# A transformer stack on one core: heads of the hybrid layers reordered, modulation pieces spread over later projections, first attention one step deeper

## The reference, cut to what matters

```python
for l, mixer in ((0, diff_attention), (1, neighbourhood_attention)):
    mod = silu(c) @ ada_w[l] + ada_b[l]          # six rows of 1024 channels, for x and for the context
    x += gate * mixer(rmsnorm(x) * (1 + scale) + shift)      # qkv, attention, wo
    x += gate * conv_ffn(rmsnorm(x) * (1 + scale) + shift)   # up, depthwise conv, silu gate, down

def _diff_attend(q, k, v, lam, subln, lam_init):  # 8 heads of two halves j
    s = jnp.einsum('bqhjd,bkhjd->bhjqk', q, k).astype(jnp.float32) * (HEAD_DIM ** -0.5)
    p = jax.nn.softmax(s, axis=-1)
    a = (p[:, :, 0] - lam * p[:, :, 1]).astype(v.dtype)
    o = jnp.einsum('bhqk,bkhe->bqhe', a, v)
    o = rmsnorm(o, subln) * (1.0 - lam_init)

for l in range(2):                                # hybrid layers
    h = rmsnorm(x, norm_g[l]); proj = h @ w_in[l]
    o = nsa_mixer, pool_mixer, conv_mixer, fox_mixer  of slices of proj
    acc = sum(sigmoid(merge[i]) * ((o[i] * silu(gates[i])) @ w_branch[i]) for i in range(4))
    x = x + acc @ w_out
```

## Time and profile before

| what | value |
|---|---|
| device time, median of 3 | 1682.14 us (1679.67 to 1682.47) |
| the profiled execution's own time | 1682.3 us |
| its span | 1680.5 us |
| mean granted clock of PE | 0.987 |
| busy PE, DVE, ACT, POOL | 1609.4, 893.8, 748.7, 539.6 us |

### The profile page before, as it was taken

One profiled execution on the slowest core, in us unless ns is written; L12 is line 12 of the kernel. 1 busy time (PEld: TensorE's weight loads), 2 busy tenths in 40 slices (PEclk: granted clock), 3 DMA queues, 4 the chain that ended last, 5 costly groups with the idle time before them and its releaser, 6 DMA issues.

```text
span 1680.5 us, 26674 instructions
## 1 busy us (share of the span) xinstructions
PE 1609.4 (96%) x10956; PEld 1404.1 (84%) x10956; DVE 893.8 (53%) x1405; ACT 748.7 (45%) x1359; POOL 539.6 (32%) x359
## 2 busy tenths in 40 slices
PE   6999988999999999999999999998999998999997
PEld 4769556778777888868968999997999998999997
DVE  3344485347523564333165788647575557568334
ACT  4323475345322343234276655445544444554443
POOL 1224144223211222220273111024424665523553
PEclk8999999999999999999999999999999999999999
DMA  9165510344255222366233454553534543533551
GB/s 395 54 228 182 204 64 1 141 147 156 68 203 201 100 77 69 121 213 230 81 76 133 151 190 160 173 177 120 196 125 155 176 168 119 201 126 131 181 191 51
DMA packets 52984, 249.39 MB, mean 148 GB/s; under 512 B 20608, under 2 KB 21760, under 8 KB 26368
## 3 DMA queue, kind: packets, MB, share of 16 engines
q1 hardware_dynamic: 44400, 244.42, 41.9%
q10 hardware_dynamic: 8464, 3.28, 0.8%
HBM read 246.63 MB, written 1.05 MB: 147 GB/s over the span
## 4 chain that ended last, share of the span: by engine, by line
PE 86%; DVE 7%; ACT 2%; DMA 2%; issue 2%; POOL 1%; SPq 0%; POOLq 0%; DVEq 0%; ACTq 0%
PE psq L529 18%; PE psq L531 17%; PE psq L530 17%; PE ps L529 6%; PE ps L531 6%; PE ps L530 6%; PE ps L542 2%; DMA RAW<-wstream 2%; PE psq L884 1%; PE psq L885 1%; PE psq L886 1%; DVE STAT L1154 1%; PE ps L1290 1%; ACT WH L501 1%; PE psq L2105 1%
## 5 line engine op out<-in xcount | busy, mean ns | idle before, releaser
L511 DVE TENSOR_TENSOR WL<-RAW,WH 128x1024 fp32r<-128x1024 f32 (+3 forms) x263 | 316.9, 1229 | 413.4 <-ACT WH L501 413.4
L529 PE MATMUL psq<-NH,WH 128*128 128x256 f32 (+1 forms) x1640 | 521.9, 318 | 13.3 <-DVE TMP L1727 10.9
L531 PE MATMUL psq<-NH,WL 128*128 128x256 f32 (+1 forms) x1640 | 515.5, 314 | 0.0
L530 PE MATMUL psq<-NL,WH 128*128 128x256 f32 (+1 forms) x1640 | 515.3, 314 | 0.0
L511 POOL TENSOR_TENSOR WL<-RAW,WH 128x1024 fp32r<-128x1024 f32 (+2 forms) x117 | 297.0, 2540 | 552.4 <-ACT WH L501 552.3
L501 ACT ACTIVATE WH<-RAW 128x1024 fp32r<-128x1024 f32 (+2 forms) x380 | 361.2, 1001 | 206.5 <-DMA RAW<-wstream 152.2
L529 PEld LDWEIGHTS psq<-NH,WH 128*128 128x128 f32 x1640 | 316.1, 193 | 42.8 <-DVE TMP L1727 11.2
L531 PEld LDWEIGHTS psq<-NH,WL 128*128 128x128 f32 x1640 | 315.7, 193 | 18.2
L530 PEld LDWEIGHTS psq<-NL,WH 128*128 128x128 f32 x1640 | 316.2, 193 | 17.3
L529 PE MATMUL ps<-NH,WH 128*128 128x256 f32 (+1 forms) x376 | 124.3, 331 | 0.0
L530 PE MATMUL ps<-NL,WH 128*128 128x256 f32 (+1 forms) x376 | 123.5, 328 | 0.0
(11 more groups left out here) (346 smaller groups left out, 2837.1 us busy)
## 6 DMA issues: line engine op xcount, KB each, us to landing
RAW<-wstream SPq DMA_DIRECT2D x196, 1024.0 KB, 4.9
RAW<-wstream SPq DMA_DIRECT2D x32, 704.0 KB, 4.1
K<-first SPq DMA_DIRECT2D x4, 1024.0 KB, 15.9
X<-xin SPq DMA_DIRECT2D x2, 1024.0 KB, 6.1
V<-first SPq DMA_DIRECT2D x2, 1024.0 KB, 19.7
Q<-first SPq DMA_DIRECT2D x2, 1024.0 KB, 25.2
BR<-rpb ACTq DMA_DIRECT2D x8, 256.0 KB, 9.0
BR<-rpb SPq DMA_DIRECT2D x8, 256.0 KB, 8.5
```

What stands on the lines that cost most here:

```text
L511: e.tensor_tensor(WL[:, u % 3, a:z], RAW[:, v % 3, a:z], WH[:, u % 3, a:z].bitcast(F32), ALU.subtract).then_inc(w_lo_p if pool else w_lo_v, 1)
L529: e.matmul(o, lh, rh, start=start, stop=False)
L530: e.matmul(o, lh, rl, start=False, stop=False)
L531: return e.matmul(o, ll, rh, start=False, stop=stop)
```

## The change

It touches orders and waits, and buffers in the first attention. (1) Start: the first row copy stands ahead of the split of unit 0, the second ahead of that of unit 1; the second part of the constants is loaded behind the fifth `first` unit. (2) First attention: jobs 0 to 3 compute scores among the last value tiles; every stage behind them has one age more (44 steps), with nine P tiles; five pieces of wo are used in its last steps. (3) Modulation units 4 to 7 of two groups stand between later projections, none in front of the first. (4) Heads of the hybrid layers: DVE copies kn right behind qn; the turns, the flats' split and the gain stand later. (5) POOL (and for two units DVE) make the last low weight parts behind low parts of activations; some wo units are split two ahead instead of three.

```diff
@@ -136,8 +136,8 @@
...
-UP_ADA = {("up", 0, 0): (0, 1, 2, 3, 4), ("up", 0, 1): (5,), ("up", 0, 2): (6,), ("up", 0, 3): (7,)}
-QKV_ADA = {("qkv", 1, 4): (0, 1, 2, 3, 4), ("qkv", 1, 5): (5,), ("qkv", 1, 6): (6,), ("qkv", 1, 7): (7,)}
+UP_ADA = {("up", 0, 0): (0, 1, 2, 3), ("up", 0, 2): (4,), ("up", 0, 3): (5,), ("up", 0, 4): (6,), ("up", 0, 5): (7,)}
+QKV_ADA = {("qkv", 1, 4): (0, 1, 2, 3), ("qkv", 1, 6): (4,), ("qkv", 1, 7): (5,), ("qkv", 1, 0): (6,), ("qkv", 1, 1): (7,)}
...
@@ -165,18 +165,18 @@
...
-    for i in range(3):
+    for i in range(2):
         add(("wo", 0, i), 1, run=False)
     for k in range(DT):
         add_ada(2, k)
         run_ada(2, k)
-    add(("wo", 0, 3), 1000, run=False)
+    for i in range(2, 4):
+        add(("wo", 0, i), 1000, run=False)
     runs += [("wo", 0, i) for i in range(4)]
     for j in range(HALF_FT):
         add(("up", 0, j), 2)
-        if j == 1:
-            for k in range(DT):
-                add_ada(3, k)
+        for k in {1: range(4), 2: (4,), 3: (5,), 4: (6,), 5: (7,)}.get(j, ()):
+            add_ada(3, k)
     for m in range(DT):
...
@@ -187,9 +187,8 @@
...
         add(("qkv", 1, i), 1000)
-        if i == 5:
-            for k in range(DT):
-                add_ada(5, k)
+        for k in {5: range(4), 6: (4,), 7: (5,), 0: (6,), 1: (7,)}.get(i, ()):
+            add_ada(5, k)
...
 
-            return SPLIT_AT[UNIT_OF[key]] + (3 if key[:2] in (("qkv", 0), ("wo", 0)) else 2)
...
                             pe_ada(e, 5, k)
-                    if u == 6:
+                    if u == 7:
...
                 for q in range(2):
-                    if l == 1 and i == 3:
-                        act_na_exp(e, q)
+                    if i == 3:
+                        (act_na_exp if l else act_diff_exp)(e, q)
                     e.wait_ge(gemm, product(key, q))
                     e.activation(V[l][:, 2 * q:2 * q + 2, 256 * i:256 * i + 256], pair(bank[b + q]),
                                  ACT.Copy).then_inc(v_sb, 1)
                 if l == 1 and i == 2:
                     e.activation(STAT[:, 11, 16:17], ONE, ACT.Exp)
-                if l == 0 or i < 3:
+                if i < 3:
                     split_hi(e, ahead(key))
...
-        DIFF_STEPS = 43
+        DIFF_STEPS = 44
...
+        def diff_p(j, i):
+
+            if i == 0:
+                return PP[:, j % 5, :]
+            return PP[:, 5 + j % 4, :] if j % 4 < 2 else TMP[:, j % 4, :]
+
+        def pe_diff_qk(e, j):
+            h, qt, k0, nk = diff_job(j)
+            if j < 2:
+                e.wait_ge(v_sb, 4 + 2 * j)
+            if j % 4 == 0:
+                e.wait_ge(qk_sb, 2 * (8 + h) + 2)
+                e.wait_ge(rot_v, 3 * (8 + h) + 3)
+            if j >= 2:
+                e.wait_ge(att_exp, 2 * (j - 1))
+            for i in range(2):
+                ps = slice(64 * i, 64 * i + 64)
+                e.matmul(bank[2 * (j % 2) + i][:, 0:nk], Q[0][ps, h, qt * P:qt * P + P], K[0][ps, h, k0:512],
+                         start=True, stop=True).then_inc(att_qk, 1)
...
             for n in range(DIFF_STEPS):
-                for age, j in each_step(n, 10, 32):
+                for age, j in each_step(n, 11, 32):
                     h, qt, k0, nk = diff_job(j)
-                    if age == 10 and qt == 3 and h < 7:
+                    if age == 11 and qt == 3 and h < 7:
                         pe_out_turn(e, h)
-                    if age == 5:
+                    if age == 6:
+                        if j == 0:
+                            e.wait_ge(v_sb, 8)
...
-                    if age == 4:
+                    if age == 5:
                         wait_mix(e, j)
+                        if j == 0:
+                            e.wait_ge(v_sb, 7)
                         if j >= 1:
...
+                    if age == 0 and j >= 4:
+                        pe_diff_qk(e, j)
...
-                if 33 <= n < 37:
+                if 33 <= n < 38:
...
+        def act_diff_exp(e, j):
+            h, qt, k0, nk = diff_job(j)
+            if j >= 4:
+                wait_mix(e, j - 4)
+            if j >= 5:
+                e.wait_ge(att_tr, j - 4)
+            e.wait_ge(att_max, j + 1)
+            for i in range(2):
+                e.activation(diff_p(j, i)[:, 0:nk], bank[2 * (j % 2) + i][:, 0:nk], ACT.Exp, bias=STAT[:, j % 8, i:i + 1],
+                             accum_out=STAT[:, j % 8, 2 + i:3 + i]).then_inc(att_exp, 1)
...
-                                         accum_out=STAT[:, j % 8, 2 + i:3 + i]).then_inc(att_exp, 1)
+                    if age == 1 and j >= 2:
+                        act_diff_exp(e, j)
...
+        def pe_last_values(e, l):
+
+            key = ("qkv", l, 11)
             v, wh, wl = weights(key)
             for q in range(4):
-                pe_na_qk(e, q)
+                (pe_na_qk if l else pe_diff_qk)(e, q)
                 if q == 0:
-                    e.wait_ge(v_sb, 10)
+                    e.wait_ge(v_sb, 8 * l + 2)
                 o = bank[4 + q // 2][:, 256 * (q % 2):256 * (q % 2) + 256]
...
                     if i == 3:
                         e.wait_ge(x_res, x_ready(1, 1))
                     if i == 0:
-                        pe_abreast(e, ("wo", l, i), [bank[b], bank[b + 1]], range(4, DT), wait_x)
+                        pe_abreast(e, ("wo", l, i), [bank[b], bank[b + 1]], range(5, DT), wait_x)
...
             n = 1 + 2 * l
             for i in range(4):
-                if l or i < 3:
-                    split_hi(e, ahead(("wo", l, i)))
+                split_hi(e, ahead(("wo", l, i)))
...
+                    last = (l, m) == (1, DT - 1)
                     for half in range(1 if l == 0 else 2):
                         key = ("down", l, c if l == 0 else half, m)
-                        split_lo(e, ahead(key), False)
+                        if not (last and half):
+                            split_lo(e, ahead(key), False)
...
                     dve_raw_lo(e, 0, DT - 1)
+                    split_lo(e, ahead(("down", 1, 1, DT - 1)), False)
...
                     for half in range(1 if l == 0 else 2):
+                        if (l, half, m) == (1, 1, DT - 1):
+                            e.wait_ge(raw_lo, 8)
                         split_lo(e, ahead(("down", l, c if l == 0 else half, m)), True)
...
             lo_prep(e, l, "qn", False)
             dve_raw_out(e, l, "qn")
+            lo_prep(e, l, "kn", False)
+            dve_raw_out(e, l, "kn")
...
         def act_head(e, l):
-            for kind in range(2):
-                if kind == 0:
-                    e.wait_ge(flat, 5 * l + 5)
-                f = FLT[:, kind, :].rearrange("p (k n) -> p k n", k=16)
-                e.activation(FHV[:, kind, :, 0, :], f, ACT.Copy).then_inc(flat_hi, 1)
             act_plain(e, l, "vn", VN[:, :, :])
...
             act_plain(e, l, "qf", QF[:, :, :], 0.125)
+            for kind in range(2):
+                if kind == 0:
+                    e.wait_ge(flat, 5 * l + 5)
+                f = FLT[:, kind, :].rearrange("p (k n) -> p k n", k=16)
+                e.activation(FHV[:, kind, :, 0, :], f, ACT.Copy).then_inc(flat_hi, 1)
             act_plain(e, l, "kf", KF[:, :, :])
...
             e.memset(FHL[:, 1024:1152].bitcast(U32), 0).then_inc(flat_lo, 1)
-            for kind in range(2):
-                f = FLT[:, kind, :].rearrange("p (k n) -> p k n", k=16)
-                e.wait_ge(flat_hi, 2 * l + kind + 1)
-                e.tensor_tensor(FHV[:, kind, :, 1, :], f, FHV[:, kind, :, 0, :].bitcast(F32),
-                                ALU.subtract).then_inc(flat_lo, 1)
-            e.memset(CM[:, 0:384].bitcast(U32), 0).then_inc(cm_zero, 1)
-            dve_turn(e, l, 0, QN[:, :, :])
-            lo_prep(e, l, "kn", False)
-            dve_raw_out(e, l, "kn")
-            dve_turn(e, l, 1, KN[:, :, :])
-            if l == 0:
-                dve_out_gain(e, 5, "nout")
             lo_prep(e, l, "vn", False)
...
             e.memset(LF[:, :, :].bitcast(U32), 0).then_inc(fx_v, 1)
+            dve_turn(e, l, 0, QN[:, :, :])
...
             e.tensor_scalar(GS, GS, 0.5, 0.5, ALU.mult, ALU.add).then_inc(gs_v, 1)
+            for kind in range(2):
+                f = FLT[:, kind, :].rearrange("p (k n) -> p k n", k=16)
+                e.wait_ge(flat_hi, 2 * l + kind + 1)
+                e.tensor_tensor(FHV[:, kind, :, 1, :], f, FHV[:, kind, :, 0, :].bitcast(F32),
+                                ALU.subtract).then_inc(flat_lo, 1)
+            e.memset(CM[:, 0:384].bitcast(U32), 0).then_inc(cm_zero, 1)
             lo_prep(e, l, "qf", False)
+            dve_turn(e, l, 1, KN[:, :, :])
             lo_prep(e, l, "kf", False)
+            if l == 0:
+                dve_out_gain(e, 5, "nout")
...
             if l == 0:
                 e.wait_ge(d_late, 16)
                 e.wait_ge(gemm, product(("down", 1, 1, 7)))
+            lo_prep(e, l, "kn", True)
             pool_turn(e, l, 0, QN[:, :, :])
```

(19 more changed lines are left out.)

68 lines of the change are left out of this document (21 added, 47 removed).

## The result

The changed kernel takes 1660.57 us (median of 4 runs, 1657.08 to 1661.6), the kernel before 1680.91 us (4 runs): the ratio is 0.9869, with a 95% interval from 0.985 to 0.9887, about 22 us less by the ratio. The profiled execution has a span of 1658.5 us, against 1680.5. That lies inside the stated range, and 12 us above the predicted 1649.

A forecast was written before the change was run, and what follows sets the result against it. PE's matmuls, busy 1609.4 of 1680.5 us, were taken to bound the kernel. Terms of -5.8, -12.3, -1.1, -8.0 and -5.5 summed to -32.7 us against 1682.3, giving 1649 us, with a range of 1638 to 1665.

The forecast's parts named there:

- the first rival: Whole kernel: attention stays at 11.05 us per head (+6.0), clock lost in the hybrid heads (+6.8); 1662 us, chance 0.20.
- The start: Row copies ahead of splits: waits -4.9, clock -3.3, new waits 2.4; sum -5.8, taken as -6 us.
- new wait for first pieces: At the start, PE arrives sooner and waits for the first units' weight pieces; put at 2.4 us.
- The first attention: Wait for first exponentials -3.3, half-clock stretch -3.0, head period 11.05 to 9.8 us for five heads -6.0; sum -12.3 us.
- I take no change there: End of the first attention: one more wo piece (k = 4) covers the last head's later chain; 0 us.
- My reason for the period: First attention: DVE's 9.93 us busy per head becomes longest, partly held by POOL, so a head takes 9.8 us.
- The norm passages: Modulation pieces no longer ahead of the projections: +0.8 after norm 1, -1.9 after norm 2; sum -1.1 us.
- The heads: Hybrid heads: kn wait of 5.51 us gone, new wait of about 4.4 at vf; -4.0 per layer, -8.0 us.
- 15, against 13.6: Hybrid heads, from vf to g1: the compress weights' split chain takes 15 us, before 13.6; g1 at 36.9.
- Before the out projection: POOL waits for the low sums, DVE's low splits shrink and all four PE waits go; -5.5 us.
- The rest at nothing: Later last splits of dve_ffn and dve_out, later wo splits, value loop with three splits: 0 us.
- The rival of the ring: Three weight buffers: modulation units between ten projections make PE wait for weights; above 1682, for example 1690 us, chance 0.02.

The follow-up runs named there:

- x7_start_old: Changed kernel with the old start: split of unit 0 ahead of the first row copy, tables' transfer behind the first weight unit; 1664.91 us, ratio to before 0.9895.
- x2_piece_back: Changed kernel with the fifth wo piece (k = 4) back behind the last step of the first attention; 1659.65 us, ratio to before 0.987.
- x1_turn_late: Changed kernel with PE turning a head's output at the end of the step in the first attention; 1660.27 us, ratio to before 0.9879.
- x8_ada_old: Changed kernel with modulation units 4 to 7 of both norm passages back in their old places; 1663.62 us, ratio to before 0.9884.
- x9_bias_sp: Changed kernel with four transfers of the second attention's bias block 1 issued by SP instead of ACT; 1657.56 us, ratio to before 0.9852.
- x5_heads_old: Changed kernel with the hybrid layers' heads in the old order on DVE, ACT and POOL; 1661.36 us, ratio to before 0.9868.
- x6_out_old: Changed kernel without POOL's wait for the low sums ahead of its weight split before the out projections; 1667.19 us, ratio to before 0.9904.
- x3_vf_early: Changed kernel with ACT's and DVE's splits of unit vf earlier in both hybrid heads; 1659.65 us, ratio to before 0.986.

## Why the prediction was right, and where its sizes were off

**The time.** The sum named 1649 and the time is 1660.57. That lies above what I called likeliest, 1641 to 1657, and nearest to the first rival's 1662; it is in the range because the range took in that rival. Of the rival's two causes one came, the clock lost in the heads, and the other did not: a head of the attention did not stay at 11.05 us. So the agreement with its number is partly luck.

**What bounds it.** Right: PE's work is unchanged, and the gain came out of waits, 19.2 of 22.0 us. The clock gave little as a whole, since the removed stretches were replaced by others: PE's busy time fell by 2.8 us, where the start and the attention alone were to give 6.3.

**The start.** Forecast -6, measured -5.6; x7_start_old confirms it at 5.7 by place. The new wait for first pieces was smaller than put (1.12 us, not 2.4), and the clock gave less back (0.84 over 14 to 35 us instead of 0.76, so 1.7 us and not 3.3).

**The first attention.** Forecast -12.3, measured -9.1 with the stretch ahead of it, 0.8 of which is the wait at 112. The wait of 3.32 us and the stretch at 0.50 are gone as forecast. The period was 10.06, where I said 9.8; that is 5.0 us for five heads instead of 6.0. The step that failed is "I take no change there": moving piece k = 4 into the last steps took a cover of 1.4 us from the last head's norm, so the wait grew from 1.07 to 2.45 us, and a stretch of 3.4 us at 0.51 came with it. x2_piece_back shows both. My reason for the period (DVE's 9.93 us of busy time) did not hold, although the number was near: that time fell to 8.51 with the change, and PE waits for POOL's norm, 1.20 us a head where it was 0.48, or in x1_turn_late for exponentials. DVE's instructions make up most of the chain there, so their order may be the limit; that is argued, not shown.

**The norm passages.** Forecast -1.1. The places of both traces say +1.1 at norm 1 (I took +0.8) and -0.9 at norm 2 (-1.9). Against x8_ada_old the spread gives 2.8, with the clock's part in it. What is missing at norm 2 is the wait of 1.30 us, ACT's hold by its own transfers, which I had not looked for; in x9_bias_sp it is gone and the passage is 2.4 us shorter than before the change.

**The heads.** The mechanism was right up to vf and the sum too large: -8.0 forecast, -2.8 measured up to g1, and 1.1 with what follows, by x5_heads_old. The kn wait went and the new one stands at vf as forecast: 4.80 us against 4.4, at 22.2 us behind vn against 21.9. I had put 4.97 us for the additions, and they took 6.93: the new order lays four of POOL's instructions over them instead of two. The term that was mis-sized is what follows the wait, "15, against 13.6": it was 17.8 in layer 0, since vf and the compress units ran partly at 0.50. I had this as part of the first rival, at 6.80 us of such a stretch for each head. In layer 0 that makes 39.9 us instead of 36.9, 3.0 of the 5.2 us that are missing up to g1. The other 2.2 are an error of the sum: I took -4.0 for layer 1 as well, from 40.9 - 36.9, but its head took only 38.05 us before:

```profile
1417.58 0.33 PE L529 MATMUL psq<-WH,NH 128*128 128x144 f32 x1 [0.35 <-DVE TMP L1727]
...
1455.63 0.33 PE L529 MATMUL psq<-NH,WH 128*128 128x256 f32 x1
```

By my own 36.9 it could give 1.15 us; it gave 1.8, to 36.3.

What that stretch costs is shown by two executions with the same head. In x1_turn_late PE waited 3.52 us at vf in layer 1, and in the changed kernel 3.55 us. In x1_turn_late the clock stayed up (vn to g1 34.3 us), in the changed kernel it fell for 6.8 us (36.3 us):

```profile
1421.00:1427.80 6.80, 6.79 (x58) 6.80 (x58) 5.75 (x7) 1.65 (x4) 2.11 (x1) 1.00 0.67 190
```

So this stretch cost 2.0 us, where I had put 3.4, and whether it comes can differ from one execution to the next. One in which PE is busy throughout costs more: 34 matmuls from 1164.30 to 1171.10 against 61 in x5_heads_old make it some 3 us, by my estimate.

**Before the out projection.** Forecast -5.5; the four waits are gone, since DVE's low splits shrank from 2.86 to 0.69 us, and x6_out_old brings both back. By places the part is worth 6.4 us.

**The rest at nothing, and the sum.** Nothing in the trace speaks against it. The rival of the ring did not come: no projection waits for weights to land (the 1.30 us above are a wait for a split), and the modulation pieces wait 2.0 us in three places, where it was 4.0. Of the 10.7 us between the sum of 32.7 and the 22.0 of the two spans, the heads are 6.9 (8.0 less 1.1) and the attention 3.2, the norms 1.3, and the start 0.2; against these the out projection gave 0.9 more. Up to g1 alone the heads' miss looks like 5.2: the rest is the clock's stretch in layer 0 that runs on to 1171 over g1's matmuls.

## What to carry to other kernels

When a wait on the busiest engine is removed, work out what arrives late next on the same chain, and price that wait with the clock that follows it, not by its length. Judge a stage at a place behind the clock's last stretch, or the gain is read too large. Do not carry a saving over from one layer to another without its own starting row. Before moving work of two engines that share operands in SBUF, count how many instructions of the one lie over those of the other: a chain of short operations pays once for each. A piece of independent work is worth what it covers, so it belongs behind the longest wait, and an engine that computes should not be the one that issues transfers while weights are streaming.

## What the runs showed of the hardware

DVE additions of 64 x 240 elements took 0.56 us alone, and 1.4 to 2.5 us when POOL's operations ran back to back; each ended 0.35 us after one of POOL's. An addition of 8 elements per row took 2.36 us in that way. DVE's subtractions of 128 x 512 elements took 2.86 us beside POOL's weight split and 0.69 us once POOL waited.

Issuing four transfers of 256 KB held ACT for 12.57 us while weights were streaming (the last one alone 9.11 us), and for 7.41 us in x8_ada_old, with the modulation units in their old places.

The clock's lower level lasted 13.6 us in x3_vf_early although PE never idled in it; PE was running the compress units and then g1 there, behind a wait of 3.35 us. Behind waits of 3.52 and 3.55 us in the same place it came in one execution and not in the other.
